# Key and value columns of the input weights loaded ahead of the query columns, and taken by token tiles 0 and 1 together

## The reference

```
h = rms_norm(x) * g1
[u | q | k | v] = h @ w_in          # widths 512 | 512 | 128 | 128
a = pool_mixer(u)                   # trailing means over 2, 4, 8, 16 tokens, a 128x128 map per group
b = attention(q, k, v)              # 8 query heads, 2 key/value heads of 64, window of two chunks of
                                    # 64 tokens, norm of q and k, slopes by distance, a sink per head
x = x + concat(a, b) @ w_out
x = x + relu(rms_norm(x) * g2 @ w_up)**2 @ w_down      # hidden width 4096
```

## Time and profile before

| | us |
|---|---|
| median of 3 runs | 864.29 (864.01 to 866.1) |
| the profiled execution | 863.61 |
| its span | 861.8 |
| TensorE busy | 856.5 (99%) |
| VectorE busy | 539.3 (63%) |
| ScalarE busy | 416.4 (48%) |
| GpSimd busy | 233.8 (27%) |

### The profile page before, as it was taken

The page is one execution under the profiler, slowest core; times in us unless marked ns, Lnnn a source line. Parts: engine busy times, 40 slices in busy tenths (PEclk is TensorE's granted clock), DMA queues, the critical chain, the costliest instruction groups (busy, mean ns, idle before and its releaser), DMA issues.

```text
span 861.8 us, 10784 instructions
## 1 busy us (share of the span) xinstructions
PE 856.5 (99%) x4062; PEld 709.0 (82%) x4062; DVE 539.3 (63%) x741; ACT 416.4 (48%) x728; POOL 233.8 (27%) x195
## 2 busy tenths in 40 slices
PE   8999999999999999999999999999999999999998
PEld 7888888888888888888888888888888888888887
DVE  7788588844477765666566566458745464646462
ACT  8865446632157555555555555534333333333330
POOL 2421201010141222234322223004543004444440
PEclk9999999999999999999999999999999999999999
DMA  9531002651011654445554442899742453242422
GB/s 349 177 124 48 26 25 74 212 204 48 26 49 50 229 174 134 135 169 178 156 170 135 135 135 94 309 373 359 264 173 94 167 190 121 98 141 96 146 99 72
DMA packets 67598, 128.37 MB, mean 149 GB/s; under 512 B 3529, under 2 KB 20187, under 8 KB 67547
## 3 DMA queue, kind: packets, MB, share of 16 engines
q1 hardware_dynamic: 67376, 127.55, 43.3%
q10 hardware_dynamic: 171, 0.14, 0.0%
HBM read 89.92 MB, written 37.75 MB: 148 GB/s over the span
## 4 chain that ended last, share of the span: by engine, by line
PE 99%; DMA 1%; DVE 0%; ACT 0%; SPq 0%; issue 0%
PE bank L1503 31%; PE bank L1505 31%; PE bank L1504 31%; PE bank L1666 1%; PE bank L1682 1%; PE bank L1516 1%; PE bank L1635 1%; DMA mem<-in_w_in 1%; PE bank L1615 0%; PE bank L1538 0%; PE bank L1529 0%; PE bank L1534 0%; DVE wgt L1075 0%; ACT wgt L680 0%; PE bank L1619 0%; PE bank L1628 0%
## 5 line engine op out<-in xcount | busy, mean ns | idle before, releaser
L1503 PE MATMUL bank<-b_op,s_op 128*128 128x512 f32 (+1 forms) x450 | 174.7, 388 | 0.0
L1504 PE MATMUL bank<-b_op,s_op 128*128 128x512 f32 (+1 forms) x450 | 174.6, 388 | 0.0
L1505 PE MATMUL bank<-b_op,s_op 128*128 128x512 f32 (+1 forms) x450 | 174.6, 388 | 0.0
L1259 DVE TENSOR_TENSOR s_op<-s_in,s_op 128x1024 fp32r<-128x1024 f32 x56 | 75.9, 1356 | 125.6 <-ACT s_op L850 125.5
L625 POOL TENSOR_TENSOR b_sum<-d_raw,d_raw 128x1024 f32<-128x1024 f32 x40 | 96.9, 2422 | 201.2 <-DVE b_op L1263 201.2
L850 ACT ACTIVATE s_op<-s_in 128x1024 fp32r<-128x1024 f32 x56 | 59.4, 1060 | 177.4 <-PE bank L1505 151.2
L1220 DVE TENSOR_TENSOR ring<-raw,ring 128x512 fp32r<-128x512 f32 x96 | 87.4, 924 | 34.0 <-ACT ring L798 32.7
L1503 PE MATMUL bank<-xs,ring 128*128 128x512 f32 x256 | 99.7, 389 | 0.0
L1505 PE MATMUL bank<-xs,ring 128*128 128x512 f32 x256 | 99.6, 389 | 0.0
L1504 PE MATMUL bank<-xs,ring 128*128 128x512 f32 x256 | 99.6, 389 | 0.0
L1503 PEld LDWEIGHTS bank<-b_op,s_op 128*128 128x128 f32 x450 | 84.5, 188 | 17.8 <-DVE b_op L1263 0.4
(11 more groups left out here) (166 smaller groups left out, 1419.5 us busy)
## 6 DMA issues: line engine op xcount, KB each, us to landing
s_in<-h_keep SPq DMA_DIRECT2D x56, 512.0 KB, 4.0
h_keep<-h_set SPq DMA_DIRECT2D x16, 1280.0 KB, 5.1
raw<-in_w_up SPq DMA_DIRECT2D x16, 1024.0 KB, 6.4
d_raw<-in_w_down SPq DMA_DIRECT2D x32, 512.0 KB, 7.7
mem<-in_x SPq DMA_DIRECT2D x16, 512.0 KB, 5.1
h_keep<-h_set SPq DMA_DIRECT2D x16, 512.0 KB, 4.6
x_keep<-mem SPq DMA_DIRECT2D x8, 512.0 KB, 3.5
mem<-x_keep SPq DMA_DIRECT2D x8, 512.0 KB, 7.1
```

The costliest lines, as they stand in the source:

```text
L1259: nc.vector.tensor_tensor(out=s_op[G % 3][:, LO], in0=s_in[G % 3], in1=s_op[G % 3][:, HI].bitcast(F32), op=ALU.subtract).then_inc(op_lo, 1)
L1503: nc.tensor.matmul(out_ap, lhs[HI], rhs[HI], start=first, stop=False, skip_group_check=chained)
L1504: nc.tensor.matmul(out_ap, lhs[HI], rhs[LO], start=False, stop=False, skip_group_check=chained)
L1505: return nc.tensor.matmul(out_ap, lhs[LO], rhs[HI], start=False, stop=last, skip_group_check=chained)
```

## The change

The weights' load is cut by columns. First come the key and value columns of all eight slices, in five loads (slices 0, 1, 2 and 3, 4 and 5, 6 and 7), with the four halves of x_T of tiles 0 and 1 among them, then the query columns, one load for each slice. ScalarE and VectorE split the pieces in the order in which they come. TensorE takes keys and values of tiles 0 and 1 slice by slice together (`first_kv`, `project_first_kv`), and then tile 0's queries (`project_first_q`); `project_kv(1)` is gone. Two spins fewer stand ahead. The steps of attention that follow stand one or two slices later in TensorE's order: tile 0's transposes and scores by one slice, the transposes of tile 1 behind two slices of the first pooling product and no longer ahead of it, `turn_rinv(0)` and `transpose_probs(0)` by one. On ScalarE, `take_rinv(0)` moves ahead of both groups of tile 0's exponentials. On VectorE `attention_low(0)` moves up by two steps. To stay within the number of semaphores, the query loads share theirs with a late set of loads (its count goes from 16 to 32), and two counters of the pooling mixer become one.

Left out below are these semaphores and the old `project_first`.

```diff
+        KV_LOADS = (range(0, 1), range(1, 2), range(2, 4), range(4, 6), range(6, 8))
-        xT_first_in = sem("xT_first_in")
+        xT_first_in = [sem(f"xT_first_in{i}") for i in range(2)]
+        w_kv_in = [sem(f"w_kv_in{i}") for i in range(len(KV_LOADS))]
...
-            def load_w_qkv(k):
-                sp.dma_start(w_qkv_stage[k], w_in_k[k][:, POOL_W:IN_W]).then_inc(w_qkv_in[k], 16)
+            def load_w_kv(i):
+                ks = KV_LOADS[i]
+                dst = w_qkv_stage[ks[0]] if len(ks) == 1 else w_kv_pair[ks[0]]
+                src = w_in_k[ks[0]] if len(ks) == 1 else w_in_pair[ks[0] // 2]
+                sp.dma_start(dst[..., KV_COLS], src[..., POOL_W + Q_W:IN_W]).then_inc(w_kv_in[i], 16)
+            def load_w_q(k):
+                sp.dma_start(w_qkv_stage[k][:, Q_COLS], w_in_k[k][:, POOL_W:POOL_W + Q_W]).then_inc(w_q_and_B22_in[k], 16)
...
-            load_xT_half(0)
-            for k in range(KH):
-                load_w_qkv(k)
-            load_xT_half(1)
-            for k in range(KH, KT):
-                load_w_qkv(k)
-            load_xT(1)
+            load_xT_half(0, 0)
+            load_w_kv(0)
+            load_w_kv(1)
+            load_xT_half(1, 0)
+            load_w_kv(2)
+            for t in range(2):
+                load_xT_half(t, 1)
+            load_w_kv(3)
+            load_w_kv(4)
+            for k in range(KT):
+                load_w_q(k)
...
-            def split_w_qkv(k):
-                sc.wait_ge(w_qkv_in[k], 16)
-                for cols in qkv_pieces(k):
-                    nc.scalar.activation(w_qkv_s[:, k, HI, cols], w_qkv_stage[k][:, cols], ACT.Copy,
-                                         scale=g1[:, k:k + 1]).then_inc(w_qkv_hi, 1)
+            def split_w_kv(k):
+                sc.wait_ge(w_kv_in[next(i for i, ks in enumerate(KV_LOADS) if k in ks)], 16)
+                nc.scalar.activation(w_qkv_s[:, k, HI, KV_COLS], w_qkv_stage[k][:, KV_COLS], ACT.Copy,
+                                     scale=g1[:, k:k + 1]).then_inc(w_qkv_hi, 1)
+            def split_w_q(k):
+                sc.wait_ge(w_q_and_B22_in[k], 16)
+                nc.scalar.activation(w_qkv_s[:, k, HI, Q_COLS], w_qkv_stage[k][:, Q_COLS], ACT.Copy,
+                                     scale=g1[:, k:k + 1]).then_inc(w_qkv_hi, 1)
...
                 if t >= 1:
                     sc.wait_ge(values_ready, t)
                     sc.wait_ge(kT_done, t)
+                else:
+                    sc.wait_ge(w_qkv_lo, 2 * KT)
                 sc.wait_ge(kv_done, t + 1)
                 sc.wait_ge(rinv_ready, t + 1)
                 nc.scalar.activation(qkv[:, Q_W:Q_W + KV_W], bank[KV_B[t]][:, 0:KV_W], ACT.Copy,
...
+            sc.wait_ge(setup_dve, COLS_READY)
+            for k in range(2):
+                split_w_kv(k)
+            x_high(1, (0,))
+            for k in range(2, KH):
+                split_w_kv(k)
+            for t in range(2):
+                x_high(t, (1,))
+            for k in range(KH, KT):
+                split_w_kv(k)
+            for k in range(KT):
+                split_w_q(k)
-            sc.wait_ge(setup_dve, COLS_READY)
-            for k in range(KH):
-                split_w_qkv(k)
-            x_high(0, (1,))
-            for k in range(KH, KT):
-                split_w_qkv(k)
-            x_high(1)
...
-            exponentials(0, (0,))
-            exponentials(0, (1,))
+            exponentials(0)
...
-            for k in range(KH):
-                split_w_qkv(k)
-            x_low(0, (1,))
+            for k in range(2):
+                split_w_qkv(k, KV_COLS)
+            x_low(1, (0,))
+            for k in range(2, KH):
+                split_w_qkv(k, KV_COLS)
+            for t in range(2):
+                x_low(t, (1,))
-                split_w_qkv(k)
-            x_low(1)
-            dve.wait_ge(w_qkv_lo, KT + 1)
+                split_w_qkv(k, KV_COLS)
+            for k in range(KT):
+                split_w_qkv(k, Q_COLS)
+            dve.wait_ge(w_qkv_lo, 2 * KT)
...
             head_norm(3)
             x_low(7)
             pooled(0, 2)
+            attention_low(0)
             pooled_low(0, 1)
             scale_u(0, 3)
-            attention_low(0)
             softmax_head(2)
             attention_low(1)
             softmax_tail(2)
...
+            def first_kv(t, k, x_part, w_part):
+                if (x_part, w_part) == (HI, HI):
+                    pe.wait_ge(xT_hi, xT_count(t, k // KH))
+                    pe.wait_ge(w_qkv_hi, qkv_count(k, KV_COLS))
+                elif x_part == LO:
+                    pe.wait_ge(xT_lo, xT_count(t, k // KH))
+                else:
+                    pe.wait_ge(w_qkv_lo, qkv_count(k, KV_COLS))
+                stop = k == KT - 1 and w_part == LO
+                last = nc.tensor.matmul(bank[KV_B[t]][:, 0:KV_W], act(x_part, k // KH, t)[:, k % KH, :],
+                                        w_qkv_s[:, k, w_part, KV_COLS], start=k == 0 and (x_part, w_part) == (HI, HI),
+                                        stop=stop)
+                if stop:
+                    last.then_inc(kv_done, 1)
+            def project_first_kv():
+                for ks in (range(2), range(2, KH), range(KH, KT)):
+                    for k in ks:
+                        first_kv(0, k, HI, HI)
+                        first_kv(0, k, LO, HI)
+                        if k >= 2:
+                            first_kv(1, k, HI, HI)
+                            first_kv(1, k, LO, HI)
+                            first_kv(0, k, HI, LO)
+                            first_kv(1, k, HI, LO)
+                    if ks == range(2):
+                        for k in ks:
+                            first_kv(0, k, HI, LO)
+                        for k in ks:
+                            first_kv(1, k, HI, HI)
+                        for k in ks:
+                            first_kv(1, k, HI, LO)
+                        for k in ks:
+                            first_kv(1, k, LO, HI)
+            def project_first_q():
+                    pe.wait_ge(w_qkv_hi, qkv_count(k, Q_COLS))
+                    for part in (HI, LO):
+                        nc.tensor.matmul(bank[Q_B[0]][:, :], act(part, k // KH, 0)[:, k % KH, :],
+                                         w_qkv_s[:, k, HI, Q_COLS], start=first and part == HI, stop=False)
+                    pe.wait_ge(w_qkv_lo, qkv_count(k, Q_COLS))
+                    last = nc.tensor.matmul(bank[Q_B[0]][:, :], act(HI, k // KH, 0)[:, k % KH, :],
+                                            w_qkv_s[:, k, LO, Q_COLS], start=False, stop=stop)
+                last.then_inc(q_done, 1)
...
-            spin(6)
-            project_first()
-            project_kv(1, range(KT))
+            spin(4)
+            project_first_kv()
+            project_first_q()
-            project_kv(2, range(3))
+            project_kv(2, range(4))
-            project_kv(2, range(3, KT))
-            project_q(2, range(4))
+            project_kv(2, range(4, KT))
+            project_q(2, range(5))
-            project_q(2, range(4, KT))
+            project_q(2, range(5, KT))
+            project_u(0, 0, range(2))
-            project_u(0, 0, range(5))
+            project_u(0, 0, range(2, 6))
-            project_u(0, 0, range(5, KT))
-            project_u(0, 1, range(5))
+            project_u(0, 0, range(6, KT))
+            project_u(0, 1, range(6))
-            project_u(0, 1, range(5, KT))
+            project_u(0, 1, range(6, KT))
```

68 lines of the change are left out of this document (24 added, 44 removed).

## The result

| | before | after |
|---|---|---|
| median, us | 864.1 (863.39 to 866.1, 20 runs) | 865.67 (864.59 to 867.24, 20 runs) |
| profiled execution, us | 863.61 | 867.09 |
| its span, us | 861.8 | 865.3 |

The changed kernel is slower: ratio 1.0018, 95% interval 1.0013 to 1.0024, or 1.6 us. The prediction said 864.1, 0.2 us less than its 864.29 for the kernel before. 865.67 lies in its range, but between its forecast and its slower rival. The profiled execution is one of the slowest of its runs. Part of its 3.5 us is its own, so the experiments are read by their medians as well as by their rows.

What follows compares the result with a forecast made beforehand. TensorE was taken as the bound, changeable only through its start up to tile 2's keys. A 0.8 us earlier start less 0.6 us of queue delay gave -0.2 us: median 864.1 us from 864.29, range 862.5 to 866.4.

Steps and rivals of the forecast that it cites:

- Smaller first load: At the start, 128 KB of weights suffice in place of 384: first matmul at 5.2 us, a gain of 0.65 us.
- The dropped spins cost nothing: Ahead of the first matmul: two fewer spins are free, since TensorE was idle 0.69 us between its spins and 5.85.
- More pieces: First weight splits on ScalarE and VectorE: 16 in place of 9, 0.9 us more on VectorE, hidden behind the DMA queue.
- What is late next: At tile 2's keys and values: the chain from tile 0's x gives the low half at 23.3 us plus D.
- D: Early DMA queue: delay of its loads, up to tile 0's x, from shorter rows; taken as 0.6 us, range 0.2 to 2.9.
- The predicted wait of TensorE: Ahead of tile 2's keys and values, for VectorE's low part: some 1.4 us plus D, or 1.3 to 2.5 us.
- margin of 0.8 us: At tile 2's keys: low half ready at 23.3 against TensorE's start at 24.09, so TensorE starts 0.8 us minus D early.
- Tile 0's scores later: Tile 0's attention behind 24 us: scaled scores come 1.0 us later, but their transposes hold by some 0.4 us.
- 1: Rival at the early DMA queue: it loses nothing, D up to 0.3, TensorE gains 0.6 us, 863.7 us; chance 0.20.
- 2: Rival at tile 2's keys: low half comes by 21.9, so the whole 2.2 us lead stays, 862.1 us; chance 0.09.
- 4: Rival in the later stage: transposes of tile 0's probabilities meet unready scores and eat the lead, 864.9 us; chance 0.07.
- 3: Slower rival, queue from 3 to 9 us: 1 KB packets at 78 ns each, D 2.9, +2.1 us, 866.4 us; chance 0.12.

Runs made afterwards that it cites:

- e17: Changed kernel with key/value columns laid out and staged side by side, front x_T and key/value columns in 5 loads in place of 9; 866.55 us, 1.0029.
- e1: Changed kernel with eight spins in place of four ahead of the first key/value matmul and eight more in TensorE's 1.6 us gap; 865.18 us, 1.0011.
- e3: Changed kernel with key/value columns laid out by the host so slices 2 to 7 are read in 2 KB rows; 865.03 us, 1.0012.
- e4: Changed kernel with the edits of e1 and e3 together: wide rows and twelve more spins; 865.35 us, 1.0012.
- e7: e1 with two of ScalarE's slope rows moved from behind the query splits to ahead of tile 1's x; 865.38 us, 1.001.
- e13: e3 with the key/value columns also staged side by side in SBUF, so that packets are of 2 KB; 865.66 us, 1.0015.
- e10: e3 with the query columns loaded in pairs of slices, two slices in one transfer; 865.87 us, 1.0016.
- e2: Kernel before, each weight slice in two loads, key/value columns then query columns, in the old order; 865.02 us, 1.0009.
- e18: Kernel before with only slices 4 to 7 split into key/value and query column loads; 864.14 us, 0.9996.
- e6: Kernel before, one load per weight slice as now but of three 1 KB pieces a row, computing other values; 865.11 us, 1.0007.
- e9: Kernel before with tile 2's x split ahead of four pooling weights on ScalarE, and the same on VectorE; 864.5 us, 0.9997.
- e12: Kernel before without the six spins between the setup and the first projection matmul; 864.38 us, 1.0001.
- e15: e9 with ten spins in place of six ahead of the first projection matmul; 864.55 us, 1.0001.
- e11: Changed kernel with tile 0's scores, the exponentials around the turned reciprocals and attention's low part where they stood before; 865.82 us, 1.0015.
- e5: Kernel before, each weight slice in two loads of 64 partitions, rows still 3 KB; 868.54 us, 1.0047.

## Why the prediction was wrong, point by point

- *Smaller first load.* Right: 5.07 for 5.2. The lead was gone one group later, which the prediction didn't ask: "So TensorE has work from 5.2 on" took an average rate of 388 to 412 GB/s for a queue that was still filling. Tile 1's first half landed at 8.09.
- *The dropped spins cost nothing.* They cost nothing as time. What the level of TensorE's clock does in the first 14 us is missing from the prediction altogether: it reads the undisturbed 0.12 us for every key/value matmul. The level is a matter of the execution as much as of the spins (13.63 to 16.32 us for the start of tile 0's queries, all with four), and no run separates its cost.
- *More pieces.* ScalarE's 16 pieces were costed as hidden behind the queue. Once it is starved at the start (3.1 us here, 3.5 in e17), its splits end at 17.8, and hiding them fails too. In e17, where x is early, they hold the squares.
- *What is late next.* The chain was right: low half at 23.3 + D, which is 7.8 us behind x's landing. In e1, e3, e4, e7 and e13 tile 2's keys start 7.8 to 7.9 us behind it. With e1, D is 1.9 (17.45 - 15.52), which gives 25.2, a shift of 1.1; its up-projection starts 1.3 late. With the profile of after, D is 2.8 and the chain gives 26.1; the other microsecond is ScalarE's wait of 0.99 for the late queries. The predicted wait of TensorE showed in e1, e4, e7, e10 and e13 (0.4 to 1.2 us), and not in the changed kernel's own profile, where TensorE came too late to wait.
- *The size of D.* The step that failed. It was composed of 0.2 for 1 KB rows, 0.3 for the queries and 0.1 for x_T, all as loss of rate at full stream, 0.6 us. Measured are 1.9 to 2.8. 1.3 of them are in x's first step already, and the main part of these is the number of small loads in the filling queue (e13 to e17: 271 to 358 GB/s, first step 15.97 to 14.84; e2 to e18: 289 to 367, 15.95 to 14.81), which has no term in the sum at all. Short packets are at most a small part: in large loads they cost 7 to 13% of the rate (e6), but making most of them 2 KB did not move the first step (15.97 in both e13 and the changed kernel). The other 0.6 to 1.5 us are the spread of a load's 16 steps, which has no term either. The far end of the range, 2.9, held D, with the wrong mechanism.
- *From D to the time.* By the chain, D of 1.9 to 2.8 puts tile 2's keys at 25.2 to 26.1, and the estimate for a typical execution is 26.0. That fits, but the base was a lucky profile: tile 2's keys start at 24.48 to 25.36 in e9, e12, e15 and e18, whose medians equal the kernel before, and not at 24.09. The margin of 0.8 us from which the prediction counted is the margin of one early execution; the 0.7 us that it added to reach the median made up for that.
- *The rule on packet size.* The Trainium skill, "DMA: Bandwidth & Descriptors", Specifications, has line rate from 512 bytes on. e6 disagrees: its 1 KB packets moved 344 GB/s for 368, 7% less, and 13% less later. Taken for these loads, that rule would have missed the 1.6 us by more than my D did.
- *Tile 0's scores later.* Right: e11.
- *Rivals.* 1 and 2 (the queue loses nothing, the lead stays) are refuted by x's landing, 4 by e11. 3 had the place (the queue from 3 to 9 us), the size (D near 2.9) and the sign, with too low a chance (0.12); its reason, 78 ns for each 1 KB packet, is refuted by e6, and by the changed kernel's own packets of 1 KB, which took 53 ns on average from 3 to 9 us.

What stays open is why many small loads in front slow the queue. SyncE's pace of 0.47 us a load can account for the stretch up to 5 us and not for the one behind it, and no run varies it by itself. What makes one step of a load straggle is open too. The 1.6 us can't be divided: e2 alone costs 0.7 (0 to 1.6), e3 and e1 come out 0.7 and 0.9 above the kernel before, and steps of a few tenths don't add, for e4 gained no more than e1 and e3 did singly. No run gives the whole 1.6 us back with the changed order kept.

## What to carry to other kernels

Cutting the first loads smaller, so that the first matmul starts earlier, buys the first matmul and can cost the rest: ask when the last load of the start lands, because the chain behind it shifts as one. Split a transfer where the queue is already full, not where it fills. Before an early engine is given credit, look at the second operand, not the first: here 0.8 us of lead turned into a wait of 1.6 us. And before a margin under a microsecond is read from one profile, look at the same start in others: here it varied by 1.3 us between kernels of the same time.

## What the runs showed of the hardware

- A queue that is being filled moves less with small loads, and not only by idle engines: 260 GB/s at 0.88 busy (128 to 256 KB) against 367 at 0.99 (384 KB); once full, loads of 256 KB move 396.
- A load lands with the last of 16 steps, and the steps can drift apart and stay so: 0.86 us for tile 0's x before, 2.33 after, where every load issued behind the straggler up to 12.4 us had 2.3 to 3.2 us between its first and last step.
- Loads over 64 partitions moved 257 GB/s at a busy share of 1.00 with 3 KB rows, where 128 partitions gave 368 (e5).
- A packet is cut by the pieces of the destination as well as of the source (e3: 2 KB rows read, 839 packets under 2 KB; e13, both contiguous: 314).
- Matmuls of 256 columns at 0.213 us, the lower level, stand in rows whose granted clock is 1.00. The spacing of starts showed the level; the granted clock did not. With the same six spins the lower level was over by 5.85 us in one execution (before) and lasted to 8.9 (e18) and 10.7 (e9) in others.
